# A transformer stack in one kernel: full-precision products of 128 columns, two small results in idle banks, an end that works bank by bank, and one split moved ahead of a tanh

## The reference

```python
for layer in range(2):
    p = split_columns(rmsnorm(x, norm_g) @ w_in)
    # mLSTM heads, gated linear attention (GLA), sparse attention (DSA) with an index that picks 64 keys a token
    y = concatenate([y_ml, y_gla, y_dsa]) @ w_out
    x = x + y
h = x
h = h + 0.5 * swiglu(rmsnorm_2(h, ffn1_norm), w_gate, w_up, w_down)      # 2816 inner columns
# attention + gMLP branches, gated, @ w_out
h = h + 0.5 * swiglu(rmsnorm_2(h, ffn2_norm), w_gate, w_up, w_down)
return rmsnorm_2(h, final_norm)      # h * rsqrt(mean(h*h) + 1e-6) * gain, in float32
```

## Time and profile before

| | |
|---|---|
| median of 3 runs | 1138.66 us (1137.09 to 1138.79) |
| profiled execution | 1136.31 us, its span 1134.5 us |
| granted TensorE clock, mean | 0.998 of full |
| PE / PEld busy | 99% / 94% of the span |
| DVE / ACT / POOL busy | 65% / 58% / 66% |

### The profile page before, as it was taken

One profiled execution on the slowest core, in us unless ns is written; L12 is line 12 of the kernel. 1 busy time (PEld: TensorE's weight loads), 2 busy tenths in 40 slices (PEclk: granted clock), 3 DMA queues, 4 the chain that ended last, 5 costly groups with the idle time before them and its releaser, 6 DMA issues.

```text
span 1134.5 us, 22331 instructions
## 1 busy us (share of the span) xinstructions
PE 1120.8 (99%) x8968; PEld 1066.2 (94%) x8968; DVE 733.8 (65%) x1261; ACT 653.8 (58%) x1089; POOL 750.8 (66%) x578
## 2 busy tenths in 40 slices
PE   9999999999999999999999999999999999999996
PEld 7788998999988799899999999999899999999996
DVE  6896644566588775265847666667669567666664
ACT  7676854575567577346646444446566447444443
POOL 6787697657488868865764656556865774646552
PEclk9999999999999999999999999999999999999999
DMA  9554354556555534545566566655644655566551
GB/s 319 181 179 130 119 182 151 171 161 205 168 168 169 168 120 151 184 139 180 169 215 202 188 221 188 198 179 178 207 148 131 205 188 166 189 217 191 192 180 38
DMA packets 63895, 199.49 MB, mean 176 GB/s; under 512 B 6992, under 2 KB 17968, under 8 KB 63792
## 3 DMA queue, kind: packets, MB, share of 16 engines
q1 hardware_dynamic: 61920, 194.99, 53.2%
q10 hardware_dynamic: 1872, 3.08, 0.8%
HBM read 196.21 MB, written 1.84 MB: 175 GB/s over the span
## 4 chain that ended last, share of the span: by engine, by line
PE 96%; DMA 1%; DVE 1%; issue 0%; ACT 0%; SPq 0%; DVEq 0%
PE ps L1665 51%; PE ps L1735 20%; PE ps L1725 14%; PE ps L1701 2%; PE ps L1893 2%; DMA par<-in_par 1%; PE ps L1987 1%; PE ps L1967 1%; PE ps L1997 1%; PE ps L1928 1%; PE ps L1988 0%; PE ps L1867 0%; PE ps L1954 0%; PE ps L1970 0%; PE ps L1845 0%
## 5 line engine op out<-in xcount | busy, mean ns | idle before, releaser
L368 POOL TENSOR_TENSOR ring<-raw,ring 128x512 fp32r<-128x512 f32 x516 | 717.8, 1397 | 358.1 <-ACT ring L483 337.0
L1665 PE MATMUL ps<-xs,ring 128*128 128x256 f32 x5040 | 598.0, 278 | 0.6 <-DVE mq L1019 0.6
L1665 PEld LDWEIGHTS ps<-xs,ring 128*128 128x128 f32 x5040 | 582.6, 188 | 5.1 <-issue 3.2
L483 ACT ACTIVATE ring<-raw 128x1024 fp32r<-128x1024 f32 x364 | 377.8, 1052 | 89.2 <-PE ps L1735 49.4
L1735 PE MATMUL ps<-ys,ring 128*128 128x256 f32 x2016 | 235.7, 276 | 0.2 <-DVE ys L1043 0.2
L1735 PEld LDWEIGHTS ps<-ys,ring 128*128 128x128 f32 x2016 | 231.7, 188 | 0.5 <-issue 0.3
L981 DVE TENSOR_TENSOR ring<-raw,ring 128x1024 fp32r<-128x1024 f32 x106 | 148.5, 1401 | 122.4 <-ACT ring L483 121.8
L1725 PE MATMUL ps<-ring,xs 128*128 128x512 f32 x672 | 164.5, 397 | 0.0
L1725 PEld LDWEIGHTS ps<-ring,xs 128*128 128x128 f32 x672 | 123.3, 188 | 26.6 <-issue 1.3
L812 ACT ACTIVATE ys<-ca 128x256 fp32r<-128x256 f32 x44 | 18.3, 416 | 94.2 <-DVE ca L1445 94.2
L1294 DVE SCALAR_TENSOR_TENSOR ca<-ps,par,ca 128x253 f32<-128x253 f32 (+2 forms) x96 | 45.9, 478 | 34.4 <-ACT ca L567 33.0
(11 more groups left out here) (274 smaller groups left out, 1011.8 us busy)
## 6 DMA issues: line engine op xcount, KB each, us to landing
raw<-in_w SPq DMA_DIRECT2D x364, 512.0 KB, 3.6
y<-bias_rows SPq DMA_DIRECT2D x6, 256.0 KB, 4.3
out_y<-y SPq DMA_DIRECT2D x4, 256.0 KB, 2.5
const<-in_const SPq DMA_DIRECT2D x1, 896.0 KB, 12.3
bias_rows<-lg ACTq DMA_DIRECT2D x1, 768.0 KB, 7.7
x<-in_x ACTq DMA_DIRECT2D x1, 512.0 KB, 4.3
x<-in_x SPq DMA_DIRECT2D x1, 512.0 KB, 6.8
dec<-in_wT ACTq DMA_DIRECT2D x1, 512.0 KB, 3.6
```

The source lines that it names most:

```text
L368: last = pool.tensor_tensor(ring[:, g % RING, 1, part], raw[:, g % RAW, part], ring[:, g % RING, 0, part].bitcast(F32), ALU.subtract)
L483: act.activation(ring[:, g % RING, 0, :], raw[:, g % RAW, :], ACT.Copy).then_inc(S["hi"], 1)
L1665: last = mm(ps[bank][:, half * T:(half + 1) * T], ring[:, slot % RING, wp, (at + k) * P:(at + k + 1) * P], rhs(k, xp), start=(first and i ...
```

## The change

1. The full-precision products of 256 and 512 columns named above are written as products of 128 columns. `gla_squares` goes ahead of `dsa_turn(1)` behind slot 30.
2. Index columns go to `ps[0]` and the forget gate to `ps[1]`. Their products wait for `early` 5 and 6. `index_logits(0)` waits for four tiles of the normalised input instead, which stood in banks 4 and 5. The waits for `iwT_ev` and `gl_x` go to slot 10, which is the next to write banks 0 and 1.
3. In both FFNs the split that stands behind the tanh of tile 2 stands ahead of it.
4. The end is rewritten. The last three output slots are multiplied bank by bank (`end_sums`): output tiles 0 to 3 get their first two parts, then the third, then tiles 4 to 7 all three. Updates, squares and products with the gain follow as the banks are done. Squares are folded by VectorE. The sum over partitions has the squares as the stationary side and one column of ones as the moving side, so the mean square stands as a column of tokens, [128, 2]; the factor is computed on two columns and spread back to a row in every partition by products with the identity. The last multiplication is three pairs on VectorE and one on GpSimd, and the stores go in the order 0, 2, 6, 4.

```diff
@@ sync: stores at the end
-            for k in range(0, KT, 2):
-                if k < KT - 2:
+            for k in (0, 2, 6, 4):
+                if k == 6:
+                    sp.wait_ge(S["last_f"], 1)
+                else:
                     sp.wait_ge(S["x_f"], FINAL_AT + k // 2 + 1)
...
@@ gpsimd: its share of the last step
-            pool.wait_ge(S["x_g"], 3)
-            pool.wait_ge(S["rms_last"], 1)
-            pool.tensor_tensor(xn[:, KT - 3, :], xn[:, KT - 3, :], rms[:, 0:T], ALU.mult).then_inc(S["last_f"], 1)
+            pool.wait_ge(S["end_xg"], 8)
+            pool.wait_ge(S["end_sb"], 1)
             pool.tensor_tensor(xn[:, KT - 2:KT, :], xn[:, KT - 2:KT, :], both(rms[:, 0:T]), ALU.mult)\
...
@@ scalar: forget_gate (vector's index_columns likewise from ps[4] to ps[0])
-                        ins = act.activation(gs[:, 0, c * T:(c + 1) * T], ps[5][:, c * T:(c + 1) * T],
+                        ins = act.activation(gs[:, 0, c * T:(c + 1) * T], ps[1][:, c * T:(c + 1) * T],
...
@@ scalar: ffn, tile(f)
-                    gate_tanh(f)
-                    next_split(p)
+                    if f == 2:
+                        next_split(p)
+                        gate_tanh(f)
+                    else:
+                        gate_tanh(f)
+                        next_split(p)
...
@@ scalar: the end
-            for k in range(KT - 3, KT):
+            def end_square(a, b):
+                act.wait_ge(S["end_x"], a // 2 + 1 if b - a == 2 else a - 2)
+                act.activation(sqs[:, a * T:b * T], x[:, a:b, :].rearrange("p a t -> p (a t)"), ACT.Square)\
+                    .then_inc(S["end_sq"], 1)
+            def end_gain(k):
                 act.activation(xn[:, k, :], x[:, k, :], ACT.Identity, scale=gains2[:, U_FIN + k:U_FIN + k + 1])\
-                    .then_inc(S["x_g"], 1)
-            factor(FINAL)
+                    .then_inc(S["end_xg"], 1)
+            end_square(0, 2)
+            end_square(2, 4)
+            for k in range(3):
+                end_gain(k)
+            end_square(4, 6)
+            end_square(6, 7)
+            end_square(7, 8)
+            for k in range(3, 5):
+                end_gain(k)
+            act.wait_ge(S["end_var"], 1)
+            step(act.activation(rms[:, 512:514], var[:, 0:2], ACT.Ln))
+            act.activation(rms[:, 512:514], rms[:, 512:514], ACT.Exp, scale=-0.5).then_inc(S["end_rms"], 1)
+            for k in range(5, 8):
+                end_gain(k)
+            act.wait_ge(S["end_ps"], 2)
+            act.activation(rms[:, 0:T], ps[6][:, 0:T], ACT.Copy).then_inc(S["end_sb"], 1)
...
@@ vector: the end, after the last ffn
-            factor(FINAL, True)
-            dve.sem_inc(S["rms_last"], 1)
-            for k in range(KT - 3):
-                ins = stt(xn[:, k, :], x[:, k, :], gains2[:, U_FIN + k:U_FIN + k + 1], rms_ps, ALU.mult, ALU.mult)
...
+            end_update(0, 2)
+            end_update(2, 4)
+            end_fold(0, 2, 2, 2).then_inc(S["end_fold"], 1)
+            end_update(4, 6)
+            dve.wait_ge(S["end_fold"], 1)
+            end_fold(0, 1, 1, 2).then_inc(S["end_fold"], 1)
+            end_fold(4, 5, 1, 3).then_inc(S["end_fold"], 1)
+            end_update(6, 7)
+            end_update(7, 8)
+            dve.wait_ge(S["ssq"], FINAL + 1)
+            mean_square(var[:, 0:2], ps[4][:, 0:2], D, S["end_var"])
+            dve.wait_ge(S["end_rms"], 1)
+            v, r = var[:, 0:2], rms[:, 512:514]
+            step(tt(v, v, r, ALU.mult))
+            step(tt(v, v, r, ALU.mult))
+            stt(r, v, -3.0, r, ALU.add, ALU.mult).then_inc(S["end_r"], 1)
+            dve.wait_ge(S["end_ps"], 1)
+            for k in range(0, KT - 2, 2):
+                dve.wait_ge(S["end_xg"], k + 2)
+                tt(xn[:, k:k + 2, :], xn[:, k:k + 2, :], both(ps[5][:, 0:T]), ALU.mult).then_inc(S["x_f"], 1)
...
@@ tensor: sum_squares; gla_squares is cut in the same way, 2 products of 512 into 8 of 128
                 for c in range(2):
-                    last = mm(ps[4][:, 0:T], ones, sqs[:, c * T:(c + 1) * T], start=(c == 0), stop=(c == 1))
+                    for a in (0, P):
+                        last = mm(ps[4][:, a:a + P], ones, sqs[:, c * T + a:c * T + a + P],
+                                  start=(c == 0 and a == 0), stop=(c == 1 and a == P), skip_group_check=True)
...
@@ tensor: index_columns (forget_gate likewise: waits early + 6, writes ps[1])
+                    pe.wait_ge(S["early"], it * EARLY + 5)
                     for tt in range(2):
-                        last = mm(ps[4][:, 8 * tt:8 * tt + 8], rows[:, tt * P:(tt + 1) * P], ident[:, 96:104],
+                        last = mm(ps[0][:, 8 * tt:8 * tt + 8], rows[:, tt * P:(tt + 1) * P], ident[:, 96:104],
...
@@ tensor: index_logits
                     if p == 0:
-                        pe.wait_ge(S["iwT_ev"], it + 1)
-                        pe.wait_ge(S["gl_x"], it + 1)
+                        pe.wait_ge(S["x_hi"], it * KT + 4)
+                        pe.wait_ge(S["x_lo"], it * KT + 4)
...
@@ tensor: ml_values (scores2 likewise: a product of 256 and one of 128 into three of 128)
-                        mm(o, lhs(0), pml[:, h % 2, 0:T], start=True, stop=False)
+                        mm(o[:, 0:P], lhs(0), pml[:, h % 2, 0:P], start=True, stop=True)
+                        mm(o[:, P:T], lhs(0), pml[:, h % 2, P:T], start=True, stop=False)
                         last = mm(o[:, P:T], lhs(1), pml[:, h % 2, T:3 * P], start=False, stop=True)
...
-                        28: [(gla_out,)], 29: [(dsa_turn, 0)], 30: [(dsa_turn, 1), (gla_squares,)],
+                        28: [(gla_out,)], 29: [(dsa_turn, 0)], 30: [(gla_squares,), (dsa_turn, 1)],
...
+                        if q == 0 and r == R_DK:
+                            pe.wait_ge(S["iwT_ev"], it + 1)
+                            pe.wait_ge(S["gl_x"], it + 1)
...
@@ tensor: the last three output tiles of the last ffn
+            def end_sums(slot, y_done):
...
+                here(slot + 1)
+                pe.wait_ge(S["y_lo"], y_done + first + 2)
+                for n in range(4):
+                    part(n, (0, 1))
+                here(slot + 2)
+                pe.wait_ge(S["y_lo"], y_done + first + 3)
+                for n in range(4):
+                    ins = part(n, (2,))
+                    if n % 2:
+                        ins.then_inc(S["end_out"], 1)
+                part(4, (0, 1, 2))
+                part(5, (0, 1, 2)).then_inc(S["end_out"], 1)
+                part(6, (0, 1, 2))
+                part(7, (0, 1, 2)).then_inc(S["end_out"], 1)
...
@@ tensor: the last sum of squares and the factor
-                    last = mm(ps[4][:, 0:T], ones, sqs[:, (2 * b + a) * T:(2 * b + a + 1) * T],
-                              start=(b == 0 and a == 0), stop=(b == N_UPDATES - 1 and a == 1))
...
+                    last = mm(ps[4][:, c:c + 1], sqs[:, k * T + c * P:k * T + (c + 1) * P], ones[:, 0:1],
+                              start=(first and c == 0), stop=(final and c == 1), skip_group_check=True)
...
+            pe.wait_ge(S["end_fold"], 3)
+            end_squares(0, first=True)
+            end_squares(4)
+            pe.wait_ge(S["end_sq"], 4)
+            end_squares(6)
+            pe.wait_ge(S["end_sq"], 5)
+            end_squares(7, final=True).then_inc(S["ssq"], 1)
+            pe.wait_ge(S["end_r"], 1)
+            for b in (5, 6):
+                for c in range(2):
+                    last = mm(ps[b][:, c * P:(c + 1) * P], rms[:, 512 + c:513 + c].broadcast_to((P, P)), ident,
+                              start=True, stop=True)
+                last.then_inc(S["end_ps"], 1)
```

More of the change, by code:

```diff
@@ L842, in ffn @@
                     early(n + 1, par2, U_MIX)
-                squares(n + 1, last)
-                if not last:
+                    squares(n + 1)
                     for p in range(at + FFN_SLOTS - 2, at + FFN_SLOTS):
@@ L1849, in forget_gate @@
                     pe.wait_ge(S["wa_in"], 16 * it + 16)
+                    pe.wait_ge(S["early"], it * EARLY + 6)
                     for c in range(2):
[L1851 removed]
+                        last = mm(ps[1][:, c * T:(c + 1) * T], wa[:, c * P:(c + 1) * P], rows, start=True, stop=True)
                     last.then_inc(S["gl_ps"], 1)
@@ L1912, in gla_squares @@
                     for c in range(2):
-                        last = mm(ps[6 + c][:, :], ones, sqs[:, c * 512:(c + 1) * 512],
-                                  start=True, stop=True)
+                        for a in range(0, 512, P):
+                            last = mm(ps[6 + c][:, a:a + P], ones, sqs[:, c * 512 + a:c * 512 + a + P],
+                                      start=True, stop=True)
                     last.then_inc(S["gssq"], 1)
```

58 lines of the change are left out of this document (36 added, 22 removed).

## The result

The changed kernel is slower: 1148.81 us (median of 4 runs, 1148.28 to 1149.00) against 1137.88 us for the kernel before on the same chip (4 runs, 1137.01 to 1138.79); ratio 1.0099, 95% interval 1.0084 to 1.0114. I had predicted 1134.5 us, 1132.5 to 1137.0.

The account below looks back on a forecast made before the run. TensorE, busy 99% of the span, was taken to bound the kernel, plus the end behind it. Gains 2.1 + 0.2 - 0.8 + 2.65 = 4.15 us, off a median of 1138.66, gave 1134.5 us, range 1132.5 to 1137.0.

Parts of the forecast that it names:

- Products of 128 columns: Cut full-precision runs on TensorE: 108 more loads and products lose some 0.8 us, bounds 0 and 1.6.
- Nothing in the rows lets it gain: On the cut full-precision products: the profile rows showed no way for the cut to save time; 0.8 us loss expected.
- The swap of `gla_squares` and `dsa_turn`: Order of gla_squares and dsa_turn(1): moves neither end of its run, delays one split wanted much later; worth nothing.
- Idle banks: Index logits in two layers: TensorE's wait at L1843 goes, 1.07 us a layer, 2.1 us gained, bounds 0 and 2.4.
- The end: Behind the last weight products: rewritten end puts the last store over at 1129.2 instead of 1131.86, 2.65 us gained, bounds 1.2 to 3.3.
- my list: Timed steps of the new end, from VectorE's updates, squares and factor to spread, last multiplication and stores, over at 1129.2.
- eight records of 128 for the spread: Step in the new end: factor spread back by eight products, from 1125.4 to the second bank ready at 1126.6.
- The split ahead of the tanh: First FFN: the slot is ready some 2 us earlier and TensorE's wait goes, 0.2 us gained, bounds 0 and 0.3.
- The slower rival: Short products' loads not hidden: some 200 records at distance 0.19 us cost 15.6 us more, 1150.1 us; chance 0.04.
- I am wrong if: Signs: short-record distance outside 0.107 to 0.115, another PE wait of about 1 us, or last weight product to span end above 11 us.
- the bounds: Sum of all terms' extremes: 0.4 us slower to 5.9 us faster, 1139.1 to 1132.8 us.

Follow-up runs that it names:

- e10: Kernel before with only the idle banks for index columns and forget gate; median 1135.23 us, ratio 0.9994.
- e9: Kernel before with the new end alone; median 1134.96 us, ratio 0.9973.
- e4: Changed kernel with one more 128-column product at the head of each of the five sums of squares; 1143.07 to 1148.77 us, ratio 1.0068.
- e6: Kernel of e1 with the tanh put ahead of the split again, as in the kernel before; 1134.79 us, ratio 0.9959.
- e7: Kernel of e1 with the split ahead of the tanh in tiles 2, 3 and 4 instead of one; 1134.13 us, ratio 0.9959.
- e8: Kernel of e7 with gla_squares cut, dsa_turn behind it, and scores2's 128-column product ahead of its 256-column one; 1132.31 us, ratio 0.9940.
- e1: Changed kernel with all four cut products (sum_squares, ml_values, scores2, gla_squares) written whole again; median 1138.07 us, ratio 0.9986.
- e12: Changed kernel with only the two sums of squares ahead of the FFNs whole; four runs 1134.81 to 1135.89 us, six 1140.30 to 1142.75, ratio 1.0018.

## Why the prediction was wrong

- **The step that failed** is "Products of 128 columns", in its sentence "All of it lies on TensorE, hence on the path. Bounds: 0 [...] and 1.6". I priced the cut runs by their own records alone. Their records cost what I read: they stand 0.112 apart. From the first record of each cut run to the second weight product behind it, all 22 runs together take 0.63 us more than before; my rows gave 0.87, which the sum took as 0.8. What I left out is that the end of such a run sets the spacing of everything behind it: 3793 more products at 117.8 ns, 16.9 us. "Nothing in the rows lets it gain" was true, but the trace of before also held what could make it lose. It has the two values itself: behind `gla_squares` 24 products stand at 117.8 ns, and I had read the mean of a line and not its spread. These products in the kernel before, then after:

```profile
124.88 3.39 PE L1665 MATMUL ps<-xs,ring 128*128 128x256 f32 x24
```

```profile
123.96 2.99 PE L1717 MATMUL ps<-xs,ring 128*128 128x256 f32 x24
```

Their first distance, 0.518 before and 0.20 after, still holds the last record of the run ahead; the other 23 take 2.71 us before and 2.61 after.

- **The swap of `gla_squares` and `dsa_turn`** "moves neither end of its run", I had written. It moved what the run ended with, and the 24 products behind went to 113.3 ns: 0.1 us a layer gained. As `gla_squares` was cut in the same runs, the effects of swap and cut aren't told apart.
- **Idle banks**, 2.1 predicted: 2.0 by e10's account, and 2.13 in the changed kernel, taken from start to start over the two index logits. The wait is gone in both layers, and nothing was given back. Right.
- **The end**, 2.65 predicted: 2.15 from the last weight product to the last issue, 2.0 by e9. Up to the start of the spread every step came within 0.1 us of my list. The step that was mis-sized is "eight records of 128 for the spread": I took them at the distance of the full clock, 1.2 us until the second bank is ready, and it took 1.7, as the clock had fallen after PE's wait of 1.31 us for the factor. Where it stayed up (e4, e6, e7, e8) the end gives 2.7.
- **The split ahead of the tanh**, 0.2 predicted. Its own size can't be told. But a stall of 0.2 us is not worth 0.2 us here: in e1 it came back 10 us later and turned the spacing; with the order of before (e6) it stands where it stood, and doesn't. I had asked what is late next at the banks and not here.
- **The slower rival** (short loads not hidden, 1150.1) is near the measured time by accident. Its distance of 0.19 us for short records is nowhere; they stand 0.112 apart.
- I had written that I am wrong if the distance of short records, a new wait or the end is off. None of the three was (the wait of 1.31 us stands inside the new end), and the time still was 14 us off: no check was put on the work that the change doesn't touch.
- A slip in the sum: the bounds add up to 2.4 + 0.3 + 3.3 = 6.0 us at most, not 5.9, so 1132.7 and not 1132.8. Nothing hangs on it.

## What to carry to other kernels

Where one kind of product fills the time, measure its start-to-start distance by stretch, ahead of and behind every other kind of run, and not its mean: here 4% on 3800 untouched products outweighed all edits. Price an insertion or a rewrite between such stretches by what it does to the spacing behind it as well, and try its other forms, one record pair more or less, or the run unsplit. A stall of 0.2 us can do the same, so take it away rather than move it. And if an engine waits shortly ahead of the last steps, read its granted clock there: here that was half a microsecond.

## What the hardware showed that I had not expected

- float32r products of 256 columns, each with a weight load of its own and at a granted clock of 1.00 in their stretches, run at 113.3 or 117.8 ns, and stay at one of the two for up to 1583 products.
- A run of full-precision products can set which. Eight short records exchange the two values (14 of 14 times), ten keep it (6 of 6), four whole ones lead to 113.3 (44 of 44); 12 and 16 went to 117.8 and 14 to 113.3, once each. For `ml_values` and for stalls the exit varied at the same value of entry.
- A wait of 1.31 us of TensorE was followed by the lower clock ahead of the next eight records (e1, e12), within them (the changed kernel, e9) or behind them (e4, e6, e7, e8); their distance is 0.112 us at the upper level and 0.214 at the lower.
- From outside one sees executions of one kernel some 6 us apart, as in e12. That the spacing parts them is not shown: only a slower one was traced.
- What in the engine holds the two values is open. A phase between the loads and the products would fit the alternation with the number of records; so would something that goes by how long the run lasts. No run here tests either.
